# Attention over memory: normalising the probabilities themselves, and turning them by transpositions

## The reference, cut to what matters

```python
def memory_cross_attention(h, mem_n, wq, wk, wv, wo):
    B, S, _ = h.shape
    M = mem_n.shape[1]
    q = (h @ wq).reshape(B, S, XATTN_HEADS, XATTN_HEAD_DIM)
    k = (mem_n @ wk).reshape(B, M, XATTN_HEADS, XATTN_HEAD_DIM)
    v = (mem_n @ wv).reshape(B, M, XATTN_HEADS, XATTN_HEAD_DIM)
    s = jnp.einsum("bshd,bmhd->bhsm", q, k).astype(jnp.float32) * XATTN_HEAD_DIM ** -0.5
    p = jax.nn.softmax(s, axis=-1).astype(h.dtype)
    o = jnp.einsum("bhsm,bmhd->bshd", p, v).reshape(B, S, D_MODEL)
    return o @ wo
```

## Time and profile before

| | us |
|---|---|
| median of 3 runs | 1863.11 |
| lowest and highest | 1862.18, 1866.37 |
| the profiled execution | 1864.27 |
| its span, first to last instruction | 1862.4 |
| busy in the span: PE, PEld | 1804.2, 1555.0 |
| busy in the span: DVE, ACT | 1407.6, 1155.6 |
| mean granted clock of PE, share of full | 0.994 |

### The profile page before, as it was taken

One profiled execution on the slowest core, in us unless ns is written; L12 is line 12 of the kernel. 1 busy time (PEld: TensorE's weight loads), 2 busy tenths in 40 slices (PEclk: granted clock), 3 DMA queues, 4 the chain that ended last, 5 costly groups with the idle time before them and its releaser, 6 DMA issues.

```text
span 1862.4 us, 29769 instructions
## 1 busy us (share of the span) xinstructions
PE 1804.2 (97%) x12558; PEld 1555.0 (83%) x12559; DVE 1407.6 (76%) x1431; ACT 1155.6 (62%) x1127; POOL 19.5 (1%) x21
## 2 busy tenths in 40 slices
PE   7999999999999998999999999999999999999996
PEld 7977789999999977797878888888888888888885
DVE  7875654544557777554889898898888988889896
ACT  6555344443344645445667777777777777777774
POOL 0000000000000000000010000000000000000000
PEclk9999999999999999999999999999999999999998
DMA  8512224356536311244899999999999999999993
GB/s 255 181 47 71 70 91 173 126 191 203 181 116 216 122 48 58 81 159 170 310 367 376 393 361 394 385 368 391 367 389 383 369 389 371 386 386 365 389 394 141
DMA packets 242477, 476.51 MB, mean 256 GB/s; under 512 B 12320, under 2 KB 88224, under 8 KB 242336
## 3 DMA queue, kind: packets, MB, share of 16 engines
q1 hardware_dynamic: 239184, 463.93, 69.2%
q0 software_dynamic: 2000, 6.83, 0.9%
q10 hardware_dynamic: 1152, 3.78, 0.5%
HBM read 468.72 MB, written 5.78 MB: 255 GB/s over the span
## 4 chain that ended last, share of the span: by engine, by line
PE 89%; DVE 7%; issue 2%; ACT 1%; DMA 1%; SPq 0%; DVEq 0%; ACTq 0%; POOLq 0%
PE ps L2404 31%; PE ps L1805 16%; PE ps L2414 15%; PE ps L1790 14%; PE ps L1827 8%; PE ps L2440 1%; PE ps L1872 1%; DVE MT L1013 1%; DVE wlo L1033 1%; DMA TMP<-token_rows,st 1%; PE ps L2395 1%; DVE MT L1016 0%; DVE TMP L1013 0%; DMA raw<-in_w_in 0%; ACT TMP L501 0%
## 5 line engine op out<-in xcount | busy, mean ns | idle before, releaser
L1033 DVE TENSOR_TENSOR wlo<-raw,whi 128x2048 fp32r<-128x2048 f32 x140 | 320.8, 2291 | 53.3 <-ACT whi L868 53.1
L868 ACT ACTIVATE whi<-raw 128x2048 fp32r<-128x2048 f32 x140 | 269.0, 1921 | 116.0 <-PE ps L2414 66.1
L1026 DVE TENSOR_TENSOR wlo<-raw,whi 128x2048 fp32r<-128x2048 f32 x85 | 194.4, 2288 | 81.1 <-ACT whi L510 81.0
L510 ACT ACTIVATE whi<-raw 128x2048 fp32r<-128x2048 f32 x85 | 162.1, 1908 | 84.2 <-PE ps L1827 31.8
L1033 DVE TENSOR_TENSOR wlo<-PT,whi 128x2048 fp32r<-128x2048 f32 x84 | 192.1, 2292 | 27.8 <-ACT whi L868 27.2
L868 ACT ACTIVATE whi<-PT 128x2048 fp32r<-128x2048 f32 x84 | 161.5, 1922 | 33.9 <-PE ps L2404 33.2
L2404 PE MATMUL ps<-whi,hE_hi 128*128 128x512 f32 x660 | 182.1, 398 | 0.0
L2404 PE MATMUL ps<-wlo,hE_hi 128*128 128x512 f32 x660 | 177.0, 390 | 0.0
L2404 PE MATMUL ps<-whi,hE_lo 128*128 128x512 f32 x660 | 176.6, 389 | 0.0
L2404 PEld LDWEIGHTS ps<-wlo,hE_hi 128*128 128x128 f32 x660 | 123.9, 188 | 26.8
L2404 PEld LDWEIGHTS ps<-whi,hE_lo 128*128 128x128 f32 x660 | 123.9, 188 | 26.3
(11 more groups left out here) (350 smaller groups left out, 3263.6 us busy)
## 6 DMA issues: line engine op xcount, KB each, us to landing
raw<-in_moe_w_up SPq DMA_DIRECT2D x111, 1024.0 KB, 7.8
PT<-in_moe_w_down SPq DMA_DIRECT2D x56, 1024.0 KB, 7.2
PT<-in_moe_w_gate SPq DMA_DIRECT2D x55, 1024.0 KB, 7.4
TMP<-in_moe_w_gate SPq DMA_DIRECT2D x55, 1024.0 KB, 7.3
raw<-in_moe_w_down SPq DMA_DIRECT2D x55, 1024.0 KB, 7.2
raw<-in_w_in SPq DMA_DIRECT2D x28, 1024.0 KB, 5.5
raw<-in_ffn_w_gate SPq DMA_DIRECT2D x11, 1024.0 KB, 5.4
raw<-in_ffn_w_up SPq DMA_DIRECT2D x11, 1024.0 KB, 5.6
```

Of the source, the lines that this page charges most:

```text
L510: nc.scalar.activation(whi[i % SPL][:, :], raw[d % RAW][:, :], ACT.Copy).then_inc(S("w_hi"), 1)
L868: nc.scalar.activation(ex_hi[m % XSPL], ex_raw[m % XRAW], ACT.Copy).then_inc(S("w_hi"), 1)
L1026: V.tensor_tensor(wlo[i % SPL][:, :], raw[d % RAW][:, :], whi[i % SPL][:, :].bitcast(F32), ALU.subtract).then_inc(S("w_lo"), 1)
L1033: V.tensor_tensor(ex_lo[m % XSPL], ex_raw[m % XRAW], ex_hi[m % XSPL].bitcast(F32), ALU.subtract).then_inc(S("w_lo"), 1)
```

## The change

DVE no longer writes scaled identities. It multiplies the probabilities themselves, in place, by the reciprocal of their sum: one instruction for each half and head, 128x256 instead of 128x128. On PE the eight products with a scaled identity in each half become transpositions with the plain identity (`tr` in place of `mm`). The tile `inv_sum` falls away. And the order on DVE changes: after the third bank's maximum the reciprocals of the first half and the multiplications of its heads 0 and 1 follow, then the fourth bank's maximum, then heads 2 and 3, then the second half's reciprocals and its four multiplications. Both layers are changed alike.

```diff
-        inv_sum = lambda i: mt(6)[:, P * i:P * i + P]
...
+                def sums(t):
+
+                    dve.wait_ge(S("at_exp"), 8 * l + NH * (t + 1))
+                    chain.link(lambda: V.reciprocal(col(ST_RS + NH * t, NH), col(ST_SUM + NH * t, NH)))
+
+                def probabilities(t, heads):
+
+                    for h in heads:
+                        ts(pr[:, t, h, :], pr[:, t, h, :], col(ST_RS + NH * t + h), ALU.mult).then_inc(S("at_p"), 1)
+
                 for b in range(4):
                     dve.wait_ge(S("at_s"), 4 * l + b + 1)
                     chain.link(lambda: V.tensor_reduce(col(ST_MX + 2 * b, 2), ps[:, b, :].rearrange("p (h n) -> p h n", h=2), AX, ALU.max))
                     ts(col(ST_MX + 2 * b, 2), col(ST_MX + 2 * b, 2), -1.0, ALU.mult).then_inc(S("at_max"), 1)
-                    if b >= 2:
-                        t = b - 2
-                        dve.wait_ge(S("at_exp"), 8 * l + NH * (t + 1))
-                        chain.link(lambda: V.reciprocal(col(ST_RS + NH * t, NH), col(ST_SUM + NH * t, NH)))
-                        for i in range(NH * t, NH * t + NH):
-                            ts(inv_sum(i), ident, col(ST_RS + i), ALU.mult).then_inc(S("at_p"), 1)
+                    if b == 2:
+                        sums(0)
+                        probabilities(0, (0, 1))
+                    if b == 3:
+                        probabilities(0, (2, 3))
+                        sums(1)
+                        probabilities(1, range(NH))
...
                     for h in range(NH):
                         pe.wait_ge(S("at_p"), 8 * l + 4 * t + h + 1)
-                        mm(ps[:, 4 + b, P * h:P * h + P], pr[:, t, h, P * m:P * m + P], inv_sum(NH * t + h)).then_inc(S("at_tr"), 1 if h == 3 else 0)
+                        tr(ps[:, 4 + b, P * h:P * h + P], pr[:, t, h, P * m:P * m + P]).then_inc(S("at_tr"), 1 if h == 3 else 0)
```

## The result

| | before | after |
|---|---|---|
| median, us | 1865.45 (20 runs) | 1867.89 (20 runs) |
| lowest and highest | 1862.18, 1868.05 | 1864.69, 1871.79 |
| profiled execution, us | 1864.27 | 1869.73 |
| its span | 1862.4 | 1867.9 |
| its mean granted clock | 0.994 | 0.989 |

The ratio is 1.0017, 95% interval 1.0011 to 1.0024: slower by about 3.2 us, where 1.6 us faster was forecast and nothing above 1865.8 was in the range. It is less than the 0.2% named as measurable, but the whole interval lies above 1. Measured here, the median of the kernel before is 2.3 us above the 1863.11 of three executions on which the forecast was built; at this ratio 1863.11 would give 1866.3, outside the range too.

What follows compares the result with a forecast made beforehand. PE, busy 97% of the span, was taken to bound the kernel. Per layer 0.51 - 0.26 + 0.54 = 0.79 us, 1.6 us in all, took the median from 1863.11 to 1861.5 us, range 1859.8 to 1865.8.

Steps and rivals of the forecast that it cites:

- Fourth maximum 0.51 us earlier: DVE, each attention: two wider multiplications replace four identities ahead of the fourth maximum, starting it at 314.45 instead of 314.96.
- Two multiplications under cover, 0.5 us left: DVE: multiplications for heads 2 and 3 fit its 1.29 us idle wait for ACT, costing nothing, with 0.5 us left.
- Wider multiplications cost 0.26 us: DVE, second half: four wider multiplications take 1.52 us, so 0.26 us of the earlier gain is lost.
- Transpositions win 0.54 us: PE, second half: the last five products take 1.09 us, five transpositions 0.55, winning 0.54 us per layer.
- First half off the path: First half's turning and ACT's copies: copies done near 318.0, wanted by PE about 319.1, so not on the path.
- nothing there stands on a clock of its own: the 1.6 us should reach the end.: Behind the attention: PE runs without a gap, waiting 1.9 us from 905 us on, so the whole gain survives.
- Rival E: Gain made but given back later where DVE or a load sets the pace: 1863.1 us, chance 0.11.
- it costs (3.4 - 1.4)/2 = 1.0 to 3.4/2 = 1.7 us, and I take the middle, 1.4: Price of one 3.4 us stretch at half clock following the thin attention stretch, more than the layer's 0.8 us gain.
- Rivals B and C: Clock falls in one attention, 1862.9 us, chance 0.26; or in both attentions, 1864.3 us, chance 0.13.
- a transposition of a 128x128 tile is one instruction: PE, second half: each transposition holds PE 0.09 to 0.11 us, where a product holds it 0.22.
- rival C: Both attentions: PE with only transpositions is granted 1.2 GHz, slowing the `vA` products; slower by 1.2 us, 1864.3, chance 0.13.

Runs made afterwards that it cites:

- push_8: Kernel before plus eight unread 128x128 products on PE in the first layer's attention, where PE waits for nothing, against the kernel before: ratio 1.0035.
- push_16: Kernel before plus sixteen unread 128x128 products on PE in the first layer's attention, where PE waits for nothing, against the kernel before: ratio 1.0032.
- before_2: Kernel before, unchanged, run once more under another label for a third profile, against the kernel before: ratio 1.0000.
- filled_2: Repeat of the full change with eight unread products on PE in each layer, against the kernel before: ratio 1.0006.
- turn_only: Multiplication in place and transpositions, but DVE's order as before, against the kernel before: ratio 1.0041.
- layer0_only: The change in the first layer only, against the kernel before: ratio 1.0009.
- filled: The full change plus eight unread products on PE in each layer, in PE's waits for DVE, against the kernel before: ratio 1.0002.
- after_aligned: The full change plus 32 already satisfied waiting instructions on PE in each layer, restoring the stream's length, against the kernel before: ratio 1.0002.
- turn_aligned: Multiplication in place and transpositions with DVE's old order, plus 32 already satisfied waiting instructions on PE in each layer, against the kernel before: ratio 1.0028.
- again: The full change run once more, against the kernel before on the same chip: ratio 1.0013, median 1868.22 against 1864.88 us.
- layer1_only: The change in the second layer only, against the kernel before: ratio 1.0006.
- turn_filled: Multiplication in place and transpositions with DVE's old order, plus eight unread products on PE in each layer, against the kernel before: ratio 1.0003.

## Why the prediction was wrong, point by point

1. *Fourth maximum 0.51 us earlier*: right, 0.52.
2. *Two multiplications under cover, 0.5 us left*: right, 0.51.
3. *Wider multiplications cost 0.26 us*: right; 1.52 us for four, as forecast, and 0.355 us was the right width.
4. *Transpositions win 0.54 us*: right within 0.1; the first `vA` product came 0.66 us after the fourth multiplication, forecast was 0.74.
5. *First half off the path*: right; PE never waits for ACT's copies.

The steps that failed:

- "nothing there stands on a clock of its own: the 1.6 us should reach the end." This is the step on which the forecast failed. It rested on PE having no gap behind the attention and on its hardly waiting from 905 us on the earlier trace rows. Both are true of the trace of before, and neither is enough. The clock falls in thin stretches hundreds of us further on, and at 711 to 718 whether it does went with when PE came there, to less than a microsecond. Rival E, "given back later", had 0.11, and only loads or DVE as mechanisms. In the profiled execution the gain of 1.7 us was followed by losses of about 7: some 2.9 at 715.7, 0.4 at the stop, 0.9 at 886 (6.8 us long instead of 3.4), 0.9 at the gathered rows, 1.6 at 961. These are read off the two profiles side by side, whose lags in the table they add up to. `push_8` against `push_16` and the pair `before_2` and `filled_2` show the mechanism for the first of them; for those at 886 and 961 it is only the same pattern.
- "it costs (3.4 - 1.4)/2 = 1.0 to 3.4/2 = 1.7 us, and I take the middle, 1.4": this took every fall to be 3.4 us long. One of 3.4 us cost 1.7 us in `turn_only` (1.24 on the `vA` products, 0.44 on the turning, 2.37 us against 1.93), the upper bound. In `layer0_only` it lasted 6.8 us, and from the third maximum to the output projection it took 16.26 us where `filled` took 13.69: 2.6 us. In `after_aligned` the fall of 3.4 us cost 1.0 us (14.70 us against the same 13.69), the lower bound. So the price was right for a fall of 3.4 us and left out the longer ones. Rivals B and C were real (`layer0_only`, `turn_only`, `turn_aligned`, `after_aligned`), but not seen in either profile of the full change. How often they occur in executions without a profile is not known.
- That "a transposition of a 128x128 tile is one instruction" was counted as time on PE only. That it also shortens the stream, and so moves the place at which PE stops for no work's sake, was not thought of. It cost 0.4 us in the profile of after and 1.2 in that of `again` (0.88 and 1.69 against 0.49), and restoring the length brought the full change from 1.0013 and 1.0017 to 1.0002, with intervals that overlap (1.0004 to 1.0022 and 1.0011 to 1.0024 against 0.9994 to 1.0011), so that this gain is not certain; in the attention of that kernel the clock still fell.
- The rule of the Trainium skill ("TensorE: Matmul & The Clock Gate", Part 4: PE-mode transpose) that a transposition does not count as busy in the same way was weighed as rival C. In the profile of after PE did nothing but transpositions, with idle times of 1.06 and 0.31 us, from 314.33 to 319.34, 5.0 us, and the clock stayed at 1.00 through them and behind, while it fell at 135.2 after 1.08 us of work in 3.4. So here they do count. Whether they count as much as their busy time says is open: in `layer0_only` the clock fell after 2.13 us, most of it transpositions, and in before it held after 2.00 us of plain products. A transposition holds PE for 0.11 us, half as long as the product that it replaces, and that alone makes the stretch thinner.

Open: why the wait for the first gathered rows was 1.9 to 2.0 us in some kernels (after, again, `layer1_only`, `turn_only`, `filled`) and 1.0 to 1.6 in the others; `filled` had 1.9 and its repeat 1.1, so it is not bound to the edit. Open too is how the 3.2 us divide between clock and stream in executions without a profile. The mean granted clock says that the clock can have most of it: 0.9915 in the executions of `again` against 0.9936 of before is 0.0021 x 1867 / 0.5 = 8 us more at half clock; at 716 such a stretch of 6.8 us cost about 2.9, so 8 us would be 3.4, an estimate. `again` lost 2.4 and had gained 1.7, so 4.1 us are to be explained.

## What to carry to other kernels

An edit of a microsecond or less may be decided not where it is made but at the next thin stretches of PE behind it: list the falls of the clock in several profiles of both kernels before believing a local gain, and try a pure shift (unread products, two sizes) as a control. Replacing products by cheaper instructions while PE waits thins it exactly where it is thinnest; in the attention of `turn_filled` and both `filled` profiles unread products put into the wait kept the clock and cost nothing. And compare the number of instructions in the stream too, since the stop near 750 us moved with it.

## What the runs showed of the hardware that was not expected

- The clock fell to 1.2 GHz for 3.4, 6.8 or 10.2 us inside the work, and within each profile all falls begin a whole number of times the shortest one's length apart. After the same work on PE it fell or held according to where that work lay against these moments: with 1.76 us more work in front there was a fall of 10.2 us, with 3.52 us more none, in one profile each. The Trainium skill ("TensorE: Matmul & The Clock Gate", Part 1: The HAM clock gate) says that the clock's bookkeeping runs freely, not started by the program; the table agrees, since the unchanged kernel had its burst at 2.63, 3.31 and 3.40.
- A stop of PE without a releaser near 750 us stands at one place in its stream and moves with the number of instructions in front: 86, 70, 102 and 118 matrix instructions are left ahead of the next wait for 0, -32, +32 and +64 instructions. It lasted 0.23 to 0.78 us at x86, 0.88 to 1.70 at x70, 1.49 and 1.93 at the others. The Trainium skill ("Runtime: NRT & Kernel Launch", Instruction fetch mechanics) says that instructions come in blocks of 16 KiB and that this is mostly hidden; the page of the profile has a queue for them with 101 packets and 1.65 MB, 16 KB each:

```profile
q8 instruction: 101, 1.65, 0.4%
```

  That this queue is the cause was not tested.
